# Decoder trunk with expert retrieval: gate arithmetic and q/k norm weights moved to ScalarE, a copy dropped, parameter waits split

## What is computed

```python
def _rms(x, g):
    y = x * lax.rsqrt(jnp.mean(x * x, axis=-1, keepdims=True) + RMS_EPS)
    return y * g
...
    qd = _rms(heads(dq), g_q_dil) * scale      # scale = HEAD_DIM ** -0.5
    kd = _rms(heads(dk), g_k_dil)
    qs = _rms(heads(bq), g_q_sb) * scale
    ks = _rms(heads(bk), g_k_sb)
...
def chunk(xc):                                  # 128 tokens; _peer
    q = (xc @ w_q).reshape(C, PEER_HEADS, 2, PEER_HALF)
    s = jnp.einsum('thpd,hpkd->thpk', q, sub_keys)
    sv, si = lax.top_k(s, PEER_TOPK)            # 16 of 128 keys, twice
    cand = sv[:, :, 0, :, None] + sv[:, :, 1, None, :]      # 256 pairs
    cidx = si[:, :, 0, :, None] * PEER_N_KEYS + si[:, :, 1, None, :]
    top, pos = lax.top_k(cand, PEER_TOPK)       # 16 of 256 pairs
    eidx = jnp.take_along_axis(cidx, pos, axis=-1)
    g = jax.nn.softmax(top, axis=-1)
    a = jnp.einsum('thkd,td->thk', u_tab[eidx], xc)
    w = g * jax.nn.gelu(a)
    return jnp.einsum('thk,thkd->td', w, v_tab[eidx])
```

## Time and profile before

| | us |
|---|---|
| median of 3 runs | 3105.1 (3103.26 to 3107.96) |
| the profiled execution | 3106.51 |
| its span | 3104.7 |
| DVE busy | 2307.4 (74%) |
| PE busy | 2457.8 (79%) |
| ACT busy | 1421.0 (46%) |
| POOL busy | 1237.1 (40%) |
| DMA moved | 1210.26 MB, mean 390 GB/s |

### The profile page before, as it was taken

The page is one execution under the profiler, slowest core; times in us unless marked ns, Lnnn a source line. Parts: engine busy times, 40 slices in busy tenths (PEclk is TensorE's granted clock), DMA queues, the critical chain, the costliest instruction groups (busy, mean ns, idle before and its releaser), DMA issues. The chain is left out here.

```text
span 3104.7 us, 28006 instructions
## 1 busy us (share of the span) xinstructions
PE 2457.8 (79%) x7696; PEld 1397.8 (45%) x7696; DVE 2307.4 (74%) x5378; ACT 1421.0 (46%) x3800; POOL 1237.1 (40%) x1028
## 2 busy tenths in 40 slices
PE   6579777897676887997787788897889888857666
PEld 5546354563354443663354444573445444322222
DVE  2496769568869998666867899667786899866665
ACT  2144634337643454335643455436683444533332
POOL 0133433333333344434444444334454444445443
PEclk9689889897788899999899998998899999988889
DMA  7399999899789999999999999999999999999998
GB/s 276 122 415 402 421 411 418 324 395 344 292 337 377 358 404 380 422 421 421 415 421 421 390 421 421 421 421 410 367 421 417 421 421 414 422 421 414 422 422 347
DMA packets 169787, 1210.26 MB, mean 390 GB/s; under 512 B 20896, under 2 KB 21152, under 8 KB 23200
## 3 DMA queue, kind: packets, MB, share of 16 engines
q0 software_dynamic: 147456, 1073.81, 84.6%
q1 hardware_dynamic: 22176, 134.66, 10.7%
HBM read 1206.29 MB, written 2.10 MB: 389 GB/s over the span
## 5 line engine op out<-in xcount | busy, mean ns | idle before, releaser
L462 POOL DMA_INDIRECT ring<-in_uv,idx x1024 | 1236.9, 1208 | 1844.5 <-PE psY L811 929.8
L811 PE MATMUL psY<-ring 128*128 128x512 f32 x3120 | 1579.0, 650 | 291.8 <-ACT ring L657 236.4
L1072 DVE CUSTOM_DVE_ANT_0 ring<-ring,htok 128x1024 f32<-128x1024 f32 x1024 | 1234.2, 1221 | 396.0 <-DMA ring<-in_uv,idx 382.0
L811 PEld LDWEIGHTS psY<-ring 128*128 128x128 f32 x3120 | 620.9, 208 | 1051.2 <-issue 1042.0
L647 ACT ACTIVATE gl<-adot 128x1 f32<-128x1 f32 x1024 | 205.1, 200 | 1055.0 <-DVE adot L1072 1032.3
L1083 DVE SCALAR_TENSOR_TENSOR x<-ring,wgt,x 128x1024 f32<-128x1024 f32 x244 | 312.3, 1280 | 24.0 <-issue 24.0
L684 PE MATMUL psP<-hT,wr 128*128 128x256 f32 (+1 forms) x1664 | 322.8, 351 | 3.8 <-ACT hT L499 3.1
L657 ACT ACTIVATE ring<-cst,wgt 128x128 f32<-128x128 f32 x780 | 313.3, 402 | 25.4
L688 PE MATMUL psP<-wr,hT 128*128 128x256 f32 x1344 | 308.0, 385 | 19.0 <-DMA wr<-in_w_out 13.6
L651 ACT ACTIVATE wgt<-gate,gl 128x1 f32<-128x1 f32 x1024 | 301.6, 295 | 33.3
L684 PEld LDWEIGHTS psP<-hT,wr 128*128 128x128 f32 x1664 | 283.8, 200 | 72.8 <-issue 39.3
(11 more groups left out here) (124 smaller groups left out, 1658.7 us busy)
## 6 DMA issues: line engine op xcount, KB each, us to landing
wr<-in_w_in SPq DMA_DIRECT2D x44, 1024.0 KB
wr<-in_w_q SPq DMA_DIRECT2D x40, 1024.0 KB
ring<-in_uv,idx POOLq DMA_INDIRECT x1024
wr<-in_w_out SPq DMA_DIRECT2D x16, 1024.0 KB
ring<-in_w_in SPq DMA_DIRECT2D x11, 1024.0 KB, 17.3
probs<-in_subkeys SPq DMA_DIRECT2D x5, 1024.0 KB
ring<-in_w_out SPq DMA_DIRECT2D x4, 1024.0 KB, 17.1
cat<-in_g_ffn SPq DMA_DIRECT2D x5, 512.0 KB, 12.6
```

What stands on the lines that cost most here:

```text
L462: pool.indirect_dma_start(out=ring[:, q % NR], out_offset=None, in_=tables[s // NC], in_offset=bass.IndirectOffsetOnAxis(ap=idx[:, s % NS, ...
L811: last = nc.tensor.matmul(psY[:, b * 512:(b + 1) * 512], ring[:, r % NR, 0:P], ring[:, r % NR, D + b * 512:D + (b + 1) * 512], start=first ...
L1072: v.tensor_tensor_reduce(out=u, in0=u, in1=htok[:, q // SLOTS % NS], scale=1.0, scalar=0.0, op0=ALU.mult, op1=ALU.add, accum_out=adot[:, J ...
```

## The change

- DVE's gate subtraction (L1029) and gate multiplication (L1047) go. The sorted values stay in `tops` (two buffers). ACT negates the largest of them into `nmax_top`, a Copy of one column with scale -1, waits for it, and takes it as the bias of the Exp. The reciprocal stays on DVE and now has a place for each head; ACT multiplies the 16 gates by it, with a Copy of scale `rsum`, at the head's first row, between the gelu and the first `wgt`. DVE's "top pairs" now waits until the Exp of the head before last is done.
- The q/k norm weights come as one small parameter `g_qk`, 128 x 4, a column for each of the four; ACT applies them as the scale of its four copies out of the transposes. DVE's multiplication L889 goes, and the scale of q is put on the 8 reciprocal roots instead of on 128x512 elements (L891).
- `norm2` writes `htok` alone; PE transposes from there, and the copy L1010 goes.
- Parameters: the two norm gains and `g_col` come first and have their own semaphore `s_gain`, which ACT awaits at `hT1`; the other three stay on `s_par`, which DVE awaits at the first "conv", "sgu in" and "sgu" of a layer. The four broadcasts of 64 values to 128 partitions go: six DMAs instead of nine.

```diff
--- before.py
+++ after.py
@@ -276,13 +276,14 @@
         si = sb("si", [P, 2, TOPK], U32)
-        top = sb("top", [P, TOPK])
+        tops = sb("tops", [P, 2, TOPK])
+        nmax_top = sb("nmax_top", [P, 1])
         pos = sb("pos", [P, 3, TOPK], U32)
         pick = sb("pick", [P, 2, TOPK])
         idx = sb("idx", [P, NS, SLOTS], I32)
         gate = sb("gate", [P, NS, SLOTS])
         gsum = sb("gsum", [P, 1])
-        rsum = sb("rsum", [P, 1])
+        rsum = sb("rsum", [P, NS, PH])
...
@@ -403,10 +405,11 @@
             def parameters(l):
-                for dst, src in ((gain_t[:, 0], g_mix), (gain_t[:, 1], g_head), (sgb, b_sgu), (cvw, conv_w)):
+                for dst, src in ((gain_t[:, 0], g_mix), (gain_t[:, 1], g_head), (g_col, g_qk)):
+                    sp.dma_start(dst[:], src[l]).then_inc(s_gain, 16)
+                for dst, src in ((sgb, b_sgu), (cvw, conv_w)):
                     sp.dma_start(dst[:], src[l]).then_inc(s_par, 16)
-                for dst, g in ((g64[:, 0], g_qd), (g64[:, 1], g_kd), (g64[:, 2], g_qs), (g64[:, 3], g_ks), (gsv, g_sgu)):
-                    sp.dma_start(dst[:], g[l].partition_broadcast(P)).then_inc(s_par, 16)
+                sp.dma_start(gsv[:], g_sgu[l].partition_broadcast(P)).then_inc(s_par, 16)
...
@@ -514,7 +517,7 @@
                 elif part == "hT1":
-                    act.wait_ge(s_par, N_PAR * (l + 1))
+                    act.wait_ge(s_gain, N_GAIN * (l + 1))
                     take_hT("hT1", s, 0, 0)
...
@@ -548,8 +551,9 @@
                         v = psT[:, n % 2].rearrange("p (a b) -> p a b", a=4)
-                        nc.scalar.activation(dq[:, j], v[:, 0:2], ACT.Copy)
-                        nc.scalar.activation(dk[:, :, c * P:(c + 1) * P], v[:, 2:4], ACT.Copy).then_inc(tp_taken, 1)
+                        nc.scalar.activation(dq[:, j], v[:, 0:2], ACT.Copy, scale=g_col[:, 2 * m:2 * m + 1])
+                        nc.scalar.activation(dk[:, :, c * P:(c + 1) * P], v[:, 2:4], ACT.Copy,
+                                             scale=g_col[:, 2 * m + 1:2 * m + 2]).then_inc(tp_taken, 1)
                 elif part == "v squares":
...
@@ -633,8 +637,10 @@
                         act.wait_ge(gate_ready, T)
-                    g = gate[:, s % NS, i * TOPK:(i + 1) * TOPK]
-                    nc.scalar.activation(g, g, ACT.Exp, accum_out=gsum[:]).then_inc(top_exp, 1)
+                    top = tops[:, T % 2]
+                    link(nc.scalar.activation(nmax_top[:], top[:, 0:1], ACT.Copy, scale=-1.0))
+                    nc.scalar.activation(gate[:, s % NS, i * TOPK:(i + 1) * TOPK], top, ACT.Exp, bias=nmax_top[:],
+                                         accum_out=gsum[:]).then_inc(top_exp, 1)
...
@@ -647,6 +653,8 @@
                         act.wait_ge(gate_ready, TOP_NO[s, J % PH] + 1)
+                        g = gate[:, s % NS, n:n + TOPK]
+                        link(nc.scalar.activation(g, g, ACT.Copy, scale=rsum[:, s % NS, J % PH:J % PH + 1]))
                     for i in range(NG):
...
@@ -727,8 +735,9 @@
                     pe.wait_ge(normed, n + 1)
+                    t = htok[:, s % NS] if part == "hT2" else hn
                     for b in range(2):
-                        transposes(BATCH_NO[part, s, 0] + b, [hn[:, (4 * b + k) * P:(4 * b + k + 1) * P] for k in range(4)])
+                        transposes(BATCH_NO[part, s, 0] + b, [t[:, (4 * b + k) * P:(4 * b + k + 1) * P] for k in range(4)])
                 elif part == "piece":
...
@@ -874,9 +883,9 @@
                 n = NORM_NO.get((part, s), 0) + 1
+                if c == 0 and part in ("conv", "sgu in", "sgu"):
+                    dve.wait_ge(s_par, N_PAR * (l + 1))
                 if part == "norm1":
-                    if c == 0:
-                        dve.wait_ge(s_par, N_PAR * (l + 1))
                     root(n, 1, D)
...
@@ -884,11 +893,10 @@
                     hv = hn[:].rearrange("p (h d) -> p h d", d=HD)
-                    link(v.tensor_tensor(hv, tmq[:, j].rearrange("p a (h d) -> p (a h) d", d=HD), per_head(rs, 16), ALU.mult))
-                    h4 = hn[:].rearrange("p (a h d) -> p a h d", a=4, d=HD)
-                    link(v.tensor_tensor(h4, h4, g64[:].unsqueeze(2).broadcast_to([P, 4, H, HD]), ALU.mult))
-                    q = hn[:].rearrange("p (a b c) -> p a b c", a=2, b=2)[:, :, 0]
-                    v.tensor_scalar(q, q, HD ** -0.5, None, ALU.mult).then_inc(qk_done, 1)
+                    q = rs[:].rearrange("p (a b h) -> p a b h", a=2, b=2)[:, :, 0]
+                    link(v.tensor_scalar(q, q, HD ** -0.5, None, ALU.mult))
+                    v.tensor_tensor(hv, tmq[:, j].rearrange("p a (h d) -> p (a h) d", d=HD), per_head(rs, 16),
+                                    ALU.mult).then_inc(qk_done, 1)
                 elif part == "bias":
...
@@ -1005,9 +1013,8 @@
                         dve.wait_ge(gain_in, 16 * (GROUP_LIST.index(GROUP_OF[s]) + 1))
-                    link(v.scalar_tensor_tensor(out=htok[:, s % NS], in0=x[:, c], scalar=rs[:, 0:1], in1=gain_f,
-                                                op0=ALU.mult, op1=ALU.mult))
-                    v.tensor_copy(hn[:], htok[:, s % NS]).then_inc(normed, 1)
+                    v.scalar_tensor_tensor(out=htok[:, s % NS], in0=x[:, c], scalar=rs[:, 0:1], in1=gain_f,
+                                           op0=ALU.mult, op1=ALU.mult).then_inc(normed, 1)
                 elif part == "top keys":
...
@@ -1021,12 +1028,12 @@
                         dve.wait_ge(vx_used, v_rows(PH * (s - NS + 1), 1))
-                    o = slice(i * TOPK, (i + 1) * TOPK)
+                    T = TOP_NO[s, i]
+                    if T >= 2:
+                        dve.wait_ge(top_exp, T - 1)
                     link(v.tensor_tensor(cand, sv[:, 0].unsqueeze(2).broadcast_to([P, TOPK, TOPK]),
                                          sv[:, 1].unsqueeze(1).broadcast_to([P, TOPK, TOPK]), ALU.add))
-                    found[0] = top16([(cand.rearrange("p a b -> p (a b)"), top, pos[:, 0], sc2)])
-
-                    mark(v.tensor_scalar(gate[:, s % NS, o], top[:], top[:, 0:1], None, ALU.subtract))
+                    found[0] = top16([(cand.rearrange("p a b -> p (a b)"), tops[:, T % 2], pos[:, 0], sc2)])
...
@@ -1042,9 +1049,7 @@
                     dve.wait_ge(top_exp, TOP_NO[s, i] + 1)
-                    g = gate[:, s % NS, i * TOPK:(i + 1) * TOPK]
-                    link(v.reciprocal(rsum[:], gsum[:]))
-                    v.tensor_scalar(g, g, rsum[:], None, ALU.mult).then_inc(gate_ready, 1)
+                    v.reciprocal(rsum[:, s % NS, i:i + 1], gsum[:]).then_inc(gate_ready, 1)
...
```

More of the change, by code:

```diff
@@ L215, in trunk @@
 def trunk(nc, x_in, cst_in, w_in, w_out, w_q, subkeys, w_sgu, b_sgu, conv_w, g_mix, g_head, g_ffn,
-          g_sgu, g_qd, g_kd, g_qs, g_ks, *rest):
+          g_sgu, g_qk, *rest):
     tables, out = rest[:DEPTH], rest[DEPTH]
@@ L235, in trunk @@
         gain_t = sb("gain_t", [P, 2, KD])
-        g64 = sb("g64", [P, 4, HD])
+        g_col = sb("g_col", [P, 4])
         gsv = sb("gsv", [P, MW])
@@ L301, in trunk @@
         s_x = [sem(f"s_x{c}") for c in range(NC)]
+        s_gain = sem("gain_t_loaded")
         s_par = sem("params_loaded")
@@ L445, in _ @@
             sp.wait_ge(s_out, 16 * NC)
-        N_PAR, N_LATE = 9 * 16, 16
+        N_GAIN, N_PAR, N_LATE = 3 * 16, 3 * 16, 16
         @block.gpsimd
@@ L1113 @@
         "g_ffn": np.asarray(g_ffn_norm),
-        "g_sgu": np.asarray(g_sgu_v), "g_qd": np.asarray(g_q_dil), "g_kd": np.asarray(g_k_dil),
-        "g_qs": np.asarray(g_q_sb), "g_ks": np.asarray(g_k_sb),
+        "g_sgu": np.asarray(g_sgu_v),
+        "g_qk": np.tile(np.stack([np.asarray(g) for g in (g_q_dil, g_k_dil, g_q_sb, g_k_sb)], axis=-1), (1, P // HD, 1)),
         "uv0": np.concatenate([np.asarray(peer_u)[0], np.asarray(peer_v)[0]], axis=1),
```

## The result

The changed kernel takes 3110.5 us in the median of 12 runs (3107.58 to 3117.06), the kernel before 3103.6 in 12 runs on the same chips. The ratio is 1.0026 (95% interval 1.0017 to 1.0034): 0.26% or about 8 us slower. The profiled execution took 3112.54, its span is 3110.7, 6.0 longer than before.

What follows compares the result with a forecast made beforehand. DMA engines bound the kernel, so time they run short of work counts. Terms -8.6 +2.5 +6 -1.5 +7 +3 +0.5 -0.5 sum to +8.4; against a median of 3105.1 that forecasts 3113.5 us, range 3094 to 3126.

Steps and rivals of the forecast that it cites:

- The start: Before the first gather: parameter waits, q/k part, norm2's copy and the subtraction bring it 8.6 us earlier (3.6 to 9.2).
- ACT's stall per head: ACT after each index: negation and table load, formerly hidden, put 1.6 us ahead of everything ACT does next.
- DVE's waits: DVE's idle time ahead of the key scores' MAX8 up some 40 us, ahead of the reciprocal some 7.
- Step 0: Searches of step 0: reciprocal 3.9 plus MAX8 waits 1.5, less 2.8 shed by DVE; taken as +2.5 us.
- step 1: Searches of step 1: 3.2 plus 6.4 of waits less 2.8 shed is 6.8; taken as +6 us.
- 560 to 960: Stretch where chains between engines set the pace: 1.5 us gained for steps 2 and 3 together (0 to 4.5).
- Steps (2,3): Searches in 960 to 1240 us: MAX8 waits of 13.3 less 5.6 shed is 7.7; taken as +7 us.
- The change of layer: Three small DMAs fewer between the gathers, -0.5 us; ending DVE's parameter wait there is worth nothing.
- Absorbed: Rival: ACT's pauses or gathers queued ahead cover the stalls, only the start's gain remains, 3096.5 us; chance 0.24.
- No difference: Rival: half of the net stalls, 9.5 of 19 us, reach the path against the gains, so 3104; chance 0.28.
- The start gives little: Rival: first weight piece lands only 1.5 us earlier, 3118.5, or 3124 with pauses; chance 0.12 including the drain rule.
- The load that still runs early: Rival: ACT's table load still runs early, about 3087 us; chance 0.03, counted within the 0.24 for faster.

Runs made afterwards that it cites:

- params_only: Kernel before with the two norm gains on their own semaphore and DVE's wait for the other seven parameters moved later, four broadcasts kept: 3099.9 us, ratio 0.9987.
- front_only: Changed kernel with both gate operations (subtraction and multiplication) back on DVE; start, q/k weights and norm2 stay changed: 3095.4 us, 0.9966 of the kernel before.
- delay2: sub_back with two chained one-column Exps behind the wait for the index, ahead of the real Exp, 0.5 us: 3095.2 us, 0.9967 of the kernel before.
- delay5: sub_back with five chained one-column Exps behind the wait for the index, ahead of the real Exp, 1.2 us: 3107.6 us, 1.0012 of the kernel before.
- early_exp: Changed kernel plus one unread Exp of a constant column per head on ACT, ahead of the waits for the index: 3089.7 us, 0.9950 of the kernel before.
- sub_back: Changed kernel with the gate subtraction back on DVE, Exp in place, no "top pairs" wait for the older Exp: 3088.6 us, 0.9949 of the kernel before.

## Why the forecast was right, step by step

The forecast was 3113.5, 8.4 slower than before. The ratio gives 8, the profiled execution 6.0, the medians 6.9. Mechanism and sign hold. How near the number came is in part luck: read as shifts against the kernel before, the stages missed by -0.9 (start), -2.4 (step 0), +1.7 (step 1), +0.5 (560 to 960), +1.3 (steps (2,3)), -0.7 (steps (4,5)) and -2.3 (steps (6,7)), where minus means faster than forecast, and these largely cancel. Against the terms of the sum, read as the shift of the changed kernel in the gathers:

- **The start, -8.6**: measured -9.5 at the first gather. The first product came 7.10 earlier, where I had 6.5 out of 1.5 to 7.1. The low end, a weight piece that lands late, did not occur here, but it did in params_only, so removing the broadcasts is what kept it away. The q/k part and `norm2` came as counted (PE's wait of 1.25 us is gone, and the one ahead of the transposes behind norm2 fell from 6.02 to 5.30). But front_only gained 11.6, so my term is 3 too small. 0.6 of this is the first product. The rest is time in which PE ran its products faster, for which the sum had no term: 22.59 us instead of 23.34 for the first 96, 15.49 instead of 16.83 for the 64 behind the retrieval norm, 5.41 instead of 5.73 for the first 32 of the queries. The changed kernel got only the first of these (22.41, then 17.09 and 6.20), see the last section.
- **ACT's stall per head, 1.6**: Exp 1.51 behind the negation and about 1.55 behind the end of the index. All 62 loads stand behind it.
- **DVE's waits**: MAX8 +42.4 against some 40, the reciprocal +6.3 against 7.
- **Step 0, +2.5, and step 1, +6**: against front_only, which leaves the gates as they were, the changed kernel lost 0.7 in step 0 (gathers 1 to 97) and 8.0 in step 1 (97 to 145). The sum is right, the split isn't. Against the kernel before it is +0.1 and +7.7. In step 1 I let only part of 6.8 count, because the slices ran full at first; all of it counted, and more.
- **560 to 960, -1.5**: -1.5 against front_only (-1.0 against the kernel before), but not for my reason. I had put it down mostly to the q/k part, and front_only, which sheds that as well, gained nothing there (+0.5). What did gain it is not settled.
- **Steps (2,3), +7**: 8.1. **Steps (4,5), +3**: 2.5. **Steps (6,7), +0.5**: -0.5. These too are against front_only. 960 to 1240 fell to 374 GB/s where I said about 375.
- **The change of layer, -0.5**: not told apart. That DVE's wait for the parameters there is worth nothing fits params_only, which is rid of it too and gained nothing in the stretch around it (-6.6 us at gather 241, -3.4 at 385, -5.9 at 745).

The net of the searches was 19 in the forecast; 1.0026 less 0.9966 is 0.60%, 18.7 us. In the profiled executions 2 us of the distance between these two kernels are PE's clock; how much of it is in the medians isn't known.

**The rivals.** "Absorbed" (3096.5) rested on gathers queued ahead as a cover. delay2 and delay5 show how far that goes: even 0.5 us per head costs 5.6 in all, though at the edge of the noise, and 1.2 us costs 19.6. "No difference" needed half of the stalls absorbed, which the table excludes. "The start gives little" fell at 13.17; its mechanism, PE waiting for the first weight piece, is what params_only shows. The load that still runs early is what early_exp is, and there it gave 3089.7 where I had estimated 3087.

**The drain.** The Trainium skill (ScalarE: Activation LUTs, What ACT_TABLE_LOAD costs) adds 1380 ns of drain to each load. After the change the load at 1176.04 is followed by the gelu at 1177.34, and the one at 1174.33 by the Exp at 1175.62: 1.30 and 1.29, no drain. By the page the change would have come to some 3145 by my estimate; the measurement decides against it.

What I had not asked is the better question: not what the change costs, but which of its five edits costs it. The forecast had the numbers (-8.6 and +19), but treated the stall as given with the change.

## What to carry to other kernels

When an instruction is put ahead of a function switch, look at which of the two carries the wait: the table load that had run in idle time here became exposed when an instruction that did not need it, a Copy, took the wait ahead of it, and one throw-away instruction of the new function ahead of the wait put it back. Price a stall between engines by its readers' slack and not by its length: with 64 heads, 0.5 us each cost about 6 us, 1.2 us each 20 and 2.4 us each 63. And when a change of many edits ends near zero, time its edits one by one, since a gain of 16 and a loss of 24 can stand in it side by side.

## What the runs showed of the hardware that I had not expected

**PE's clock rises at different moments of the start.** The 64 products behind the first retrieval norm took 17.09 us in the changed kernel and 15.59 in sub_back, though they start within 0.4 us of each other. The two timelines:

```profile
88.47 17.09 PE L696 MATMUL psP<-ring,hT 128*128 128x256 f32 x64 [1.47 <-ACT hT L506]
```
```profile
88.86 15.59 PE L693 MATMUL psP<-ring,hT 128*128 128x256 f32 x64 [1.47 <-ACT hT L505]
```

and the stretch 90 to 95 in each (the third value from the end is the granted clock):

```profile
90.00:95.00 5.00, 5.00 (x14) 3.94 (x13) 0.00 (x0) 0.00 (x0) 0.00 (x0) 0.54 0.16 67
```
```profile
90.00:95.00 5.00, 5.00 (x20) 4.23 (x19) 0.42 (x1) 0.00 (x0) 0.00 (x0) 0.81 0.28 118
```

Up to 90 both stand at 0.50, the 1.2 GHz level, after stretches in which PE mostly waited; at 95 both are at 1.0, 2.4 GHz. In between the changed kernel stayed low for longer. No gate has been computed by then, so it has nothing to do with the edit that differs. The next products, the first 32 of the queries, repeat it: 6.20 us at a granted clock of 0.65 in 115 to 120, where sub_back took 5.46 at 0.92. In the kernel before the 64 products took 16.83:

```profile
97.96 16.83 PE L688 MATMUL psP<-ring,hT 128*128 128x256 f32 x64 [1.47 <-ACT hT L503]
```

In the eleven kernels in which these products start between 88 and 93 us they took 15.49 to 17.09. delay5, with 16.15, had its first gather late too (-9.4, where delay2 had -11.0), but only 0.5 us of this are these products: 1.0 comes from the very first 96, which took 23.89 against 22.89, though the granted clock reads 1.00 for both in 13 to 30. So 1 to 2 us of every early reading are PE's pace, and what sets the moment at which the clock rises, or the pace of the first 96, is open.

**Small loads among gathers.** At the change of layer DVE stood still for 10.75 us in the kernel before, for the last of nine small parameters:

```profile
1243.73 0.15 DVE L840 TENSOR_SCALAR nt<-ss 128x1 f32<-128x1 f32 x1 [10.75 <-DMA gsv<-in_g_sgu]
```
```profile
1232.00:1245.00 13.00, 1.16 (x3) 0.19 (x1) 2.05 (x9) 0.90 (x3) 1.59 (x2) 0.68 1.02 422
```

The second row is the stretch around it: DMA went on at 422 GB/s, and removing the wait gained nothing that can be seen. Ten idle us of an engine were covered there by gathers already under way, while 1.5 us in every head were not.
